# Second attention of a two-block transformer kernel: values as the stationary operand, transposed probabilities moving, outputs by features in two column groups

## The reference, cut to what matters

```python
def second_block(x, ...):
    h = rms_norm_2(x, norm1_g)
    p = h @ w_in                            # q, k, v: 512 columns each; conv and pool inputs
    q, k = rms_norm_2(q, q_norm_g), rms_norm_2(k, k_norm_g)
    y_attn = chunked_band_attention(q, k, v, rel_bias)
    ...
    mix = concatenate([y_attn, y_conv, y_pool])      # 512 + 256 + 256 columns
    x = x + mix @ w_out
    x = x + square(relu(rms_norm_2(x, norm2_g) @ w_mlp1)) @ w_mlp2

def chunked_band_attention(q, k, v, rel_bias):
    scores = q @ k.T * d ** -0.5 + bias     # chunks of 64, the own one and 8 before it
    p = softmax(scores)
    out = p @ v
```

## Time and profile before

| | |
|---|---|
| median of 3 runs | 1455.87 us (1450.27 to 1456.78) |
| profiled execution, its own time | 1452.82 us |
| its span in the profile | 1451.1 us |
| PE busy | 1398.9 us, 96% |
| DVE busy | 679.5 us, 47% |
| ACT busy | 546.0 us, 38% |
| POOL busy | 659.1 us, 45% |
| second attention, step 0 to the first matmul of the attention's half of the output product | about 968 to 1063 us |

### The profile page before, as it was taken

One profiled execution on the slowest core, in us unless ns is written; L12 is line 12 of the kernel. 1 busy time (PEld: TensorE's weight loads), 2 busy tenths in 40 slices (PEclk: granted clock), 3 DMA queues, 4 the chain that ended last, 5 costly groups with the idle time before them and its releaser, 6 DMA issues.

```text
span 1451.1 us, 17537 instructions
## 1 busy us (share of the span) xinstructions
PE 1398.9 (96%) x6751; PEld 1163.2 (80%) x6751; DVE 679.5 (47%) x991; ACT 546.0 (38%) x792; POOL 659.1 (45%) x523
## 2 busy tenths in 40 slices
PE   2999999999999989999999998999999999999999
PEld 2887787888888878888888876877888888888887
DVE  6677968766622882141325456346514214132131
ACT  0635453576554163141332325324425214133231
POOL 0543855332233855445445544841144544544442
PEclk9999999999999999999999999999999999999999
DMA  9353346633214333232232232320022232223222
GB/s 332 109 146 89 88 146 185 194 118 115 88 31 145 120 90 112 92 107 91 87 116 87 87 116 77 99 87 30 30 88 87 87 103 100 87 88 114 87 92 82
DMA packets 126552, 153.29 MB, mean 106 GB/s; under 512 B 5564, under 2 KB 89808, under 8 KB 126496
## 3 DMA queue, kind: packets, MB, share of 16 engines
q1 hardware_dynamic: 123760, 146.95, 31.9%
q0 software_dynamic: 2192, 5.49, 1.1%
q10 hardware_dynamic: 544, 0.10, 0.0%
HBM read 150.32 MB, written 2.21 MB: 105 GB/s over the span
## 4 chain that ended last, share of the span: by engine, by line
PE 87%; DVE 6%; POOL 3%; ACT 2%; issue 1%; DMA 1%; SPq 0%; DVEq 0%; POOLq 0%; ACTq 0%
PE bank L1558 25%; PE bank L1560 25%; PE bank L1559 25%; PE bank L1703 3%; POOL w_lo L520 2%; PE bank L1693 2%; DVE tmp L1126 1%; PE bank L2050 1%; DMA arena<-in_w_ada_dram 1%; PE bank L1678 1%; PE bank L1874 1%; PE bank L1818 1%; PE bank L1875 1%; ACT w_hi L675 1%; PE bank L1668 1%
## 5 line engine op out<-in xcount | busy, mean ns | idle before, releaser
L520 POOL TENSOR_TENSOR w_lo<-raw,w_hi 128x512 fp32r<-128x512 f32 x428 | 585.6, 1399 | 679.6 <-ACT w_hi L675 678.5
L1558 PE MATMUL bank<-w_hi,a_hi 128*128 128x512 f32 x928 | 365.4, 394 | 13.0 <-DVE a_lo L1037 6.0
L1560 PE MATMUL bank<-w_hi,a_lo 128*128 128x512 f32 x928 | 362.6, 391 | 0.0
L1559 PE MATMUL bank<-w_lo,a_hi 128*128 128x512 f32 x928 | 362.4, 390 | 0.0
L675 ACT ACTIVATE w_hi<-raw 128x2048 fp32r<-128x2048 f32 x107 | 204.8, 1914 | 349.6 <-PE bank L1560 346.6
L1558 PE MATMUL bank<-a_hi,w_hi 128*128 128x512 f32 x800 | 315.6, 394 | 3.4 <-DVE a_lo L1037 2.5
L1560 PE MATMUL bank<-a_hi,w_lo 128*128 128x512 f32 x800 | 312.1, 390 | 0.0
L1559 PE MATMUL bank<-a_lo,w_hi 128*128 128x512 f32 x800 | 312.0, 390 | 0.0
L1558 PEld LDWEIGHTS bank<-w_hi,a_hi 128*128 128x128 f32 x928 | 175.1, 189 | 51.6 <-POOL w_lo L520 6.5
L1560 PEld LDWEIGHTS bank<-w_hi,a_lo 128*128 128x128 f32 x928 | 174.9, 189 | 37.1
L1559 PEld LDWEIGHTS bank<-w_lo,a_hi 128*128 128x128 f32 x928 | 175.2, 189 | 35.5
(11 more groups left out here) (231 smaller groups left out, 1190.1 us busy)
## 6 DMA issues: line engine op xcount, KB each, us to landing
raw<-in_w_mlp_dram SPq DMA_DIRECT2D x32, 1024.0 KB, 5.1
raw<-in_w_in_dram SPq DMA_DIRECT2D x24, 1024.0 KB, 5.2
arena<-in_w_ada_dram SPq DMA_DIRECT2D x18, 1024.0 KB, 5.4
raw<-in_w_ff_in_dram SPq DMA_DIRECT2D x16, 1024.0 KB, 5.3
raw<-in_w_ff_out_dram SPq DMA_DIRECT2D x16, 1024.0 KB, 5.0
raw<-in_w_out_dram SPq DMA_DIRECT2D x12, 1024.0 KB, 5.1
raw<-in_w_in_dram SPq DMA_DIRECT2D x16, 512.0 KB, 5.2
arena<-in_w_ada_dram SPq DMA_DIRECT2D x3, 2048.0 KB, 17.9
```

The costliest lines, as they stand in the source:

```text
L520: last = pool.tensor_tensor(w_lo[:, u0 % 2, cols], raw[:, u0 % 2, cols], w_hi[:, u0 % 2, cols].bitcast(F32), ALU.subtract)
L1558: pe.matmul(out_, hi_a, hi_b, start=start, stop=False)
L1559: pe.matmul(out_, hi_a, lo_b, start=False, stop=False)
L1560: return pe.matmul(out_, lo_a, hi_b, start=False, stop=stop)
```

## The change

The value product of the second attention is turned round. The stationary operand is v (128 keys by 64 features), the moving one is the transposed probabilities, 128 or 256 columns at a time: seven matmuls a head. Out come 64 features by 128 tokens for each of the four query blocks. Query blocks 0 and 3 (side 0) go to partitions 0 to 63 of bank 3, blocks 1 and 2 (side 1) to partitions 64 to 127, so the two sides use different column groups of the PE array. As the row sums lie along the moving columns now, the probabilities are divided by their sums first (`scale_rows`: a reciprocal and four `tensor_scalar` on DVE, ahead of PE's transposes, which wait for `p_scaled` in place of `p_made`). The outputs come out as the output product wants them; ACT copies each side from the bank into `a_hi` (`att_halves`), DVE subtracts to make `a_lo` (`att_rest`). `att2`, its 16 transposes, ACT's four `turned_hi` and DVE's `split_turned` of four tiles go, and the row half takes no waits by tile any more. ACT's `hi(U_WO3 + 1)` keeps its place after the loop.

```diff
+        def band_part(buf, h, side):
+            return buf[own(h % 2), h // 2].rearrange("p (q n) -> p q n", q=TB)[:, (slice(0, 4, 3), slice(1, 3))[side]]
+        def band_out(side):
+            return bank[3][own(side), 256:512].rearrange("p (q n) -> p q n", q=2)
...
@@ ACT
+            def att_halves(h):
+                act.wait_ge(o_mm, 16 + h + 1)
+                for side in range(2):
+                    act.activation(band_part(a_hi[1], h, side), band_out(side), ACT.Copy).then_inc(att_hi, 1)
             for s in range(10):
                 if s >= 2:
                     copy_probT(16 + s - 2, prob2T)
...
                     probabilities(16 + s - 1, score, prob2[:, (s - 1) % 2])
+                if s >= 2:
+                    att_halves(s - 2)
                 if s in (2, 3):
                     mix_hi(s - 2)
...
             hi(U_WO3 + 1)
-            for k in range(4):
-                turned_hi(R_ATT2, 1, k, k, 1.0)
...
@@ DVE
+            def scale_rows(h):
+                dve.wait_ge(p_made, 4 * (16 + h) + 4)
+                link(dve.reciprocal(rinv[:, 1], rsum[:, h % 2]))
+                for q in range(TB):
+                    rows_ = prob2[:, h % 2, QO[q]:QO[q] + (q + 1) * P]
+                    last = dve.tensor_scalar(rows_, rows_, rinv[:, 1, q:q + 1], None, ALU.mult)
+                last.then_inc(p_scaled, 1)
+            def att_rest(h):
+                for side in range(2):
+                    dve.wait_ge(att_hi, 2 * h + side + 1)
+                    dve.tensor_tensor(band_part(a_lo[1], h, side), band_out(side), band_part(a_hi[1], h, side).bitcast(F32), ALU.subtract).then_inc(o_made if side else att_lo, 1)
...
                     mix_lo(s - 4)
+                if 1 <= s < 9:
+                    scale_rows(s - 1)
                 if s >= 2:
-                    h = s - 2
-                    output(16 + h, att2[:, :, h * HD:h * HD + HD])
+                    att_rest(s - 2)
                 if s < 8:
                     dve.wait_ge(s_mm, 16 + s + 1)
                     add_relative(s)
...
-            split_turned(T_MIX + 4, 1, lambda k: 1.0, range(4))
...
@@ PE, probs_t
-                pe.wait_ge(p_made, 4 * h + 4)
+                if h < 16:
+                    pe.wait_ge(p_made, 4 * h + 4)
+                else:
+                    pe.wait_ge(p_scaled, h - 15)
...
                             pe.wait_ge(o_made, h)
+                            if h > 16:
+                                pe.wait_ge(att_lo, h - 16)
...
+            def band_values(h):
+                pe.wait_ge(pt_made, 3 * (16 + h) + 3)
+                blocks = prob2T.rearrange("p (b n) -> p b n", n=P)
+                out_ = [band_out(side) for side in range(2)]
+                for k in range(TB):
+                    v = qkv2[:, 2, k, h * HD:h * HD + HD]
+                    if k == 0:
+                        pe.matmul(out_[0], v, blocks[:, 0:7:6], start=True, stop=False)
+                        pe.matmul(out_[1], v, blocks[:, 1:4:2], start=True, stop=False)
+                    else:
+                        last = pe.matmul(out_[0][:, 1], v, blocks[:, 6 + k], start=False, stop=k == 3)
+                        if k == 1:
+                            pe.matmul(out_[1], v, blocks[:, 2:5:2], start=False, stop=False)
+                        elif k == 2:
+                            pe.matmul(out_[1][:, 1], v, blocks[:, 5], start=False, stop=True)
+                last.then_inc(o_mm, 1)
...
                 if s >= 2:
-                    h = s - 2
-                    values(16 + h, prob2T, lambda k: qkv2[:, 2, k, h * HD:h * HD + HD])
+                    band_values(s - 2)
...
-            pe.wait_ge(pt_made, 3 * 24)
+            pe.wait_ge(att_lo, H2)
             pe.wait_ge(o_made, 24)
-            turn(att2, 4)
-            row_half(U_WO3, 1, 1, 1, 0, False, True, lambda kk: T_MIX + 4 + kk + 1)
-            pe.wait_ge(a_lo_made, T_MIX + 8)
+            row_half(U_WO3, 1, 1, 1, 0, False, True)
```

More of the change, by code:

```diff
@@ L91 @@
 T_MIX = T_N2 + 8
-T_N3 = T_MIX + 8
+T_N3 = T_MIX + 4
 T_HID2 = T_N3 + 8
 M_H, M_X1, M_HID1, M_N2, M_MIX, M_HID2 = 0, 8, 16, 48, 56, 60
-R_H, R_SSM, R_ATT, R_X1, R_N2, R_ATT2, R_N3 = 0, 8, 16, 24, 32, 40, 44
+R_H, R_SSM, R_ATT, R_X1, R_N2, R_N3 = 0, 8, 16, 24, 32, 40
 ATT_BANKS = (6, 7, 2, 3, 6, 7, 4, 5)
@@ L209, in build @@
         prob2T = view(6656, 1280)
-        att2 = view(0, TB, 512)
         ident = sb("ident", [P, P])
@@ L280, in build @@
         cum_hi = sem("cum_hi")
+        p_scaled, att_hi, att_lo = sem("p_scaled"), sem("att_hi"), sem("att_lo")
         s_mm, mx_made, p_made = sem("s_mm"), sem("mx_made"), sem("p_made")
@@ L1480, in _ @@
             head_norm()
+            def scale_rows(h):
[8 more added lines that the diff above has]
+                    dve.wait_ge(att_hi, 2 * h + side + 1)
+                    dve.tensor_tensor(band_part(a_lo[1], h, side), band_out(side), band_part(a_hi[1], h, side).bitcast(F32), ALU.subtract)                        .then_inc(o_made if side else att_lo, 1)
             def read_cp(n):
```

## The result

| | before | changed |
|---|---|---|
| median of 10 runs | 1450.70 us (1450.27 to 1458.20) | 1460.22 us (1456.67 to 1465.30) |
| profiled execution, span | 1451.1 us | 1460.5 us |
| ratio to before, 95% interval | | 1.0049 (1.0032 to 1.0066) |

The kernel became 0.5% slower: about 7 us by the ratio. The time that was forecast, 1459.3 us, is 0.9 us from the median, but it was set on the median of the first three runs of before, 1455.87. Ten runs put that at 1450.70, so the *change* that was forecast, +3.5 us, is half of what was measured (the two medians lie 9.5 us apart; both kernels' runs scatter over some 8 us, and the ratio is not the quotient of the medians).

What follows compares the result with a forecast made beforehand. PE time and PE's waits were taken to bound the kernel. Terms 2.9 - 1.9 + 1.3 + 1.5 - 0.3 = +3.5 us, set on the three-run median 1455.87, gave 1459.3 us; own range 1457 to 1462, 8-in-10 range 1453 to 1467.

Steps and rivals of the forecast that it cites:

- Values: PE's value product in the second attention: a head takes 1.54 instead of 2.18 us, with 0.15 for entering the narrow form.
- full halving: Rival: a head's values take 1.06 us with no entry cost; sum +0.6 us, 1456.5 us; chance 14%.
- Step 1 to 2: Head 0's scaling stands behind read_cp(2) on DVE, so PE waits 1.5 us to transpose the scaled rows.
- Step 2 to 3: Head 1's scaling stands behind read_pool(0) on DVE; its transposes end 2.9 us late in all, PE idling about 3 us.
- Steps 3 to 5: Middle attention steps: scaling is hidden in steps of 9 us or more, PE keeps three times 0.64: -1.9 us.
- Steps 6 and 7: Copies, mix_hi, mix_lo and scaling take 3.6 us against 2.35 of scores; PE waits 1.3 us twice, net +1.3.
- Step 8: Head 7 is scaled after 7.7 us against 5.5 of PE work; PE waits 2.1 us, net +1.5.
- Tail: After the last values: 2.0 us of transposes go, PE waits 2.35 for weights split behind att_halves(7); net -0.3 with 0.64 saved.
- Behind the tail: Everything after the attention is the same PE-bound feed-forward, which only passes the shift on: no added time.
- clock falls: Rival: PE's waits bring one or two falls to the 1.2 GHz level, 1.7 us each; 1461 to 1463 us; chance 22%.
- In turn: Rival: the two column groups' value passes run one after another, 2.32 us a head; +8.2 us, 1464 us; chance 28%.
- faster: Case: waits on scaling and weights don't show, PE's own saving of 11 us stands; 1445 us; chance 4%.

Runs made afterwards that it cites:

- weights_later: The changed kernel with ACT's w_hi of U_WO3, and so POOL's w_lo of it, in step 6 instead of 5; 1456.60 us, ratio 1.0020 to before.
- tail kernel: The changed kernel with ACT's w_hi of U_WO3 + 1 moved ahead of the last two output copies; 1457.46 us, ratio 1.0045 to before.

## Why the prediction was right, and where not

The time fell in the forecast's range, and each place where PE would wait was named rightly. But the forecast stood on paired groups and no fall of the clock; the groups did pair, and there were four falls. In size, by its own steps, with positions counted from the first relative-bias product (transposes' end for heads 0 and 1, their start from head 4 on):

- **Values, -0.64 a head:** mis-sized. From the start of the last projection pass to that of the first score pass it took 1.55 us (1003.41 to 1004.96), and 2.50 at the same place before, so 0.95 were saved. The step that failed is "passes start in program order": PE takes the pass of the free group, so the groups pair fully (1.39 was forecast for the 14 passes, 1.23 came). The entry cost of 0.15 was right (0.32 us to the first narrow pass in place of 0.23, and 0.05 in the second). The *full halving* rival had the pairing but no entry cost, and the forecast the entry cost but not the full pairing.
- **Step 1 to 2, wait 1.5:** 1.32.
- **Step 2 to 3, 2.9 late in all:** 2.8 late (transposes of head 1 ended 40.66 us from the start of the stretch, before 37.86). The idle was 1.6 and not 3, since a passage at half clock had slowed the work ahead of it. As the lateness came out as forecast, that fall cost nothing.
- **Steps 3 to 5, -1.9:** -2.8, three times 0.95, no waits.
- **Steps 6 and 7, +1.3:** +3.5, the largest miss. Step 7's wait was 1.31 as forecast, step 6's 2.58. The sum gave DVE's convolution its old duration, when POOL's 5 us on the weights now run beside it, as ACT's copies of the outputs pushed them there; weights_later shows 1.4 us of the wait to be this. The sum put this term at nothing, although its own rows held a sign of it: the longest of the 16 tensor_scalars of 256 columns in the earlier trace rows took 1.458 us against a median of 0.354, and in the trace of before it ran beside POOL's `w_lo`. The rest is PE at half clock, of which 2.8 us fell on work.
- **Step 8, +1.5:** +1.8; the wait was 0.95 instead of 2.1, as PE ran at half clock just ahead of it. In the tail kernel, where it didn't, the wait is 2.52.
- **Tail, -0.3:** -0.4; the wait of 2.35 was 2.32, in the order ACT, POOL, PE that was given.
- **Behind the tail, 0:** +1.6, the fourth passage at half clock, in the first output matmuls.

2.8 - 2.8 + 3.5 + 1.8 - 0.4 + 1.6 = 6.5 us, which is the 6.4 of the stretch but for rounding. The forecast's mechanism and the *clock falls* rival (22%) came together: the sum's own waits caused them. The threshold that the rival took from two rows (no fall after 1.65 us of idle, a fall after 2.52) was too kind, for here the clock fell after 1.3 us; nor is the length of the wait a rule, for it didn't after head 1's 1.63. *In turn* fell with the rows of L1738 and L1739. The *faster* case fell as it said it would, by the 3.6 us behind the values and the 7.85 of the tail.

The nearness of 1459.3 to 1460.22 is luck in good part: the median of three runs of before stood 5 us over that of ten, which made up for the 3.6 us that the sum lacked (7.1 by the ratio, less 3.5). In the sum itself, too, errors of opposite sign met: 0.3 us too little saved per head, against two causes that it left out, the clock and the contention with POOL.

What stays open: when a wait brings a fall of the clock, since at waits of like length (head 6's 1.31 us in the changed kernel and in the tail kernel) it came in one execution and not in the other; and what would be won by giving the scaling to ACT, which no run tried.

## What to carry to other kernels

A matmul form that saves PE time pays only if the work it moves to the other engines fits into *their* queues: sum up DVE's and ACT's load step by step, and where an engine is already full, reordering only moves the wait. When a copy is put into a queue ahead of the split of a weight unit, follow the chain behind it to the matmul that needs the weights, and see what then runs beside it. Count short PE waits at more than their length, because each can bring a passage at half clock with it. And when a row gives the lowest, middle and longest duration of an operation, ask what ran beside the longest before pricing with the middle one.

## What the runs showed of the hardware

- Two column groups of 64 run fp32 passes side by side in full: starts under 10 ns apart, 14 passes in 1.23 us, where ten matmuls (20 passes) of 64 columns took 2.27. PE doesn't start the passes of different groups strictly in program order: with side 0 written first, side 1's first pass started three passes early. So "in order" did not hold for PE across the two groups. The Trainium skill, TensorEngine Tiling (Key Properties), has the tiles independent and a drain at a change of mode. By the first the trace agrees; at the change it shows 0.09 us more to the first narrow pass and 0.05 in the second.
- PE's clock fell to the 1.2 GHz level at four of the six waits of the changed kernel (1.3, 2.6, 1.3 and 2.3 us, not at 1.6 and 1.0), and at none where PE was kept busy until waits of 0.3 to 1.4 us were left. A fall just ahead of a wait costs little: head 1's transposes came 2.8 us late with one ahead of them, as the sum without it had it.
- Many of DVE's operations within SBUF stretch beside POOL, though not all: 0.17 to 1.21, 0.49 to 1.40, 0.69 to 1.71, four together 1.27 to 2.73 us. Its work on the banks did not: three 128x256 additions into a bank took 1.08 us beside POOL and without.
